# A transformer block kernel: the row buffers of its matmuls begin at other offsets from the weights, modulo 256 bytes

## The reference

```python
for l in range(DEPTH):                                   # DEPTH = 2
    need_ctx = l < DEPTH - 1                             # the context is carried on in layer 0 alone
    m  = silu(c) @ w_mod[l] + b_mod[l]                   # shifts, scales and gates
    o, oc = mix(modulate(x, g_mix[l]), modulate(xc, g_mix[l]), ...)
    x = x + gt1 * o
    x = x + gt2 * swiglu(modulate(x, g_ffn[l]), w_ffn_in[l], w_ffn_out[l])
    if need_ctx: ...                                     # the same for xc
return rmsnorm(x, g_final)

def mix(h, hc):                                          # four branches, gated and summed
    a_b, a_c, a_u, q, k, v, r_g, r_u, d_v, d_g, gl = split(h @ w_in)
    ys = (short_conv(a_b, a_c, a_u) @ w_a_out,  window_attention(q, k, v, kc, vc) @ w_b_out,
          (gelu(r_g) * rglru(conv(r_u))) @ w_c_out,  conformer_conv(d_v, d_g) @ w_d_out)
    return (sum_n sigmoid(gl_n) * ys_n) @ w_out
```

## Time and profile before

| | |
|---|---|
| median of three runs | 1960.27 us (1960.24 to 1960.73) |
| the profiled execution | 1960.5 us |
| its span, first instruction to last | 1958.7 us |
| granted TensorE clock, mean over the span | 0.997 |
| TensorE busy | 1930.0 us, 99% |
| VectorE, ScalarE, GpSimd busy | 72%, 46%, 41% |

### The profile page before, as it was taken

How to read it: one execution, slowest core, us unless ns; L and a number is a source line. 1 busy time by engine, 2 the same in 40 slices (tenths; PEclk the granted TensorE clock), 3 DMA queues, 4 the chain that set the end, 5 groups by cost and what they waited for, 6 DMA issues and landing times.

```text
span 1958.7 us, 29316 instructions
## 1 busy us (share of the span) xinstructions
PE 1930.0 (99%) x11006; PEld 1671.1 (85%) x11006; DVE 1416.5 (72%) x2475; ACT 908.0 (46%) x1439; POOL 812.0 (41%) x353
## 2 busy tenths in 40 slices
PE   7999999999999999999999999999999999999998
PEld 5778888888888888887888888878899999999998
DVE  5896666677789868798885544689788787645455
ACT  5787544232223343345222223599854435565443
POOL 1002322344444444344344444301647886454432
PEclk9999999999999999999999999999999999999999
DMA  8222211222232235534455442322334554544543
GB/s 344 86 86 81 92 65 65 85 88 107 86 105 88 100 138 216 192 129 170 174 219 192 190 175 83 140 78 106 130 108 151 180 186 174 193 172 172 194 174 127
DMA packets 38701, 276.25 MB, mean 141 GB/s; under 512 B 4416, under 2 KB 4416, under 8 KB 6336
## 3 DMA queue, kind: packets, MB, share of 16 engines
q1 hardware_dynamic: 38592, 274.77, 38.2%
HBM read 273.70 MB, written 1.05 MB: 140 GB/s over the span
## 4 chain that ended last, share of the span: by engine, by line
PE 81%; DVE 13%; ACT 3%; issue 2%; DMA 0%; POOL 0%; SPq 0%; DVEq 0%; ACTq 0%; POOLq 0%
PE PS L592 80%; DVE PS L1545 3%; DVE TMP L1542 1%; DVE TMP L1545 1%; ACT WH L1023 1%; DVE TMP L1548 1%; PE PS L905 1%; DVE S L1545 1%; ACT PS L1023 1%; DVE PS L1542 1%; DVE SM L1991 1%; DVE HL L1545 0%; DVE TMP L1864 0%; DVE ZL L1542 0%; DVE WL L1542 0%
## 5 line engine op out<-in xcount | busy, mean ns | idle before, releaser
L535 POOL TENSOR_TENSOR WL<-RAW,WH 128x1024 fp32r<-128x1024 f32 (+1 forms) x337 | 802.8, 2400 | 1122.9 <-ACT WH L1023 1122.9
L1023 ACT ACTIVATE WH<-RAW 128x1024 fp32r<-128x1024 f32 (+1 forms) x416 | 414.4, 1043 | 606.0 <-PE PS L592 571.4
L592 PE MATMUL PS<-HH,WH 128*128 128x512 f32 (+2 forms) x1968 | 680.7, 346 | 7.3 <-POOL WL L535 3.2
L592 PE MATMUL PS<-HH,WL 128*128 128x512 f32 (+2 forms) x1968 | 667.5, 339 | 0.0
L592 PE MATMUL PS<-HL,WH 128*128 128x512 f32 (+2 forms) x1968 | 666.9, 340 | 0.3 <-DVE HL L1545 0.3
L592 PE MATMUL PS<-ZH,WH 128*128 128x512 f32 (+1 forms) x1312 | 442.1, 337 | 3.7 <-DVE HL L1542 2.9
L592 PE MATMUL PS<-ZH,WL 128*128 128x512 f32 (+1 forms) x1312 | 441.0, 336 | 0.0
L592 PE MATMUL PS<-ZL,WH 128*128 128x512 f32 (+1 forms) x1312 | 439.3, 337 | 0.3 <-POOL ZL L559 0.3
L592 PEld LDWEIGHTS PS<-HH,WH 128*128 128x128 f32 x1968 | 373.0, 190 | 55.8 <-issue 8.2
L592 PEld LDWEIGHTS PS<-HL,WH 128*128 128x128 f32 x1968 | 372.6, 190 | 44.0 <-issue 3.8
L592 PEld LDWEIGHTS PS<-HH,WL 128*128 128x128 f32 x1968 | 373.0, 190 | 41.3
(11 more groups left out here) (210 smaller groups left out, 1740.3 us busy)
## 6 DMA issues: line engine op xcount, KB each, us to landing
RAW<-in_stream SPq DMA_DIRECT2D x200, 1024.0 KB, 4.8
CD<-in_modw SPq DMA_DIRECT2D x22, 1024.0 KB, 7.1
G<-in_modw SPq DMA_DIRECT2D x22, 1024.0 KB, 6.9
RAW<-in_stream SPq DMA_DIRECT2D x8, 768.0 KB, 4.2
CD<-in_lruw SPq DMA_DIRECT2D x2, 2048.0 KB, 11.7
X<-in_xT SPq DMA_DIRECT2D x2, 1024.0 KB, 7.1
S<-in_modw SPq DMA_DIRECT2D x2, 1024.0 KB, 12.9
RAW<-in_modw SPq DMA_DIRECT2D x1, 1024.0 KB, 19.8
```

What stands on the lines that cost most here:

```text
L535: nc.gpsimd.tensor_tensor(WL[:, a:b], RAW[:, a:b], WH[:, a:b].bitcast(F32), ALU.subtract)\
L592: return nc.tensor.matmul(out, lhs, rhs, start=start, stop=stop)
L1023: return nc.scalar.activation(out, in_, f, **kw)
```

## The change

The buffers are allocated in another order, and the second slot of `WH`, `WL` and `RAW` begins 8 words (32 bytes) later: `SLOT = SLAB + 8`, and `s * SLOT` wherever the code had `s * SLAB`. Small buffers (`PADA`, `BD2`, `AMP`, `EPST`) stand between the large ones. The offset of the rows from the weights thus becomes 64 bytes (`HH`, `HL`) or 224 bytes (`ZH`, `ZL`) where the slab is even, and 32 or 192 bytes where it is odd. No instruction is added, removed or moved on any of the five engines: apart from the shift of every line number by one, their programs read alike.

```diff
 SLAB = KC * 2 * P
+SLOT = SLAB + 8
 HALF = SLAB // 2
...
         MOD = sb("MOD", 2 * 48)
-        X = sb("X", KC * NT)
-        WH = sb("WH", 2 * SLAB, F32R)
-        WL = sb("WL", 2 * SLAB, F32R)
+        WH = sb("WH", SLOT + SLAB, F32R)
+        PADA, PADR = sb_and_rounded("PADA", 2 * GW)
+        WL = sb("WL", SLOT + SLAB, F32R)
+        BD2 = sb("BD2", KC)
+        HH = sb("HH", KC * UROW, F32R)
+        AMP = sb("AMP", 2 * 2 * KC)
+        HL = sb("HL", KC * UROW, F32R)
+        EPST = sb("EPST", 2)
         ZH = sb("ZH", KC * NT, F32R)
         ZL = sb("ZL", KC * NT, F32R)
-        HH = sb("HH", KC * UROW, F32R)
-        AMP = sb("AMP", 2 * 2 * KC)
-        SELB = sb("SELB", 32)
-        LC = sb("LC", 2 * 16)
-        HL = sb("HL", KC * UROW, F32R)
+        X = sb("X", KC * NT)
         S, SR = sb_and_rounded("S", KC * NT)
         CD = sb("CD", KC * NT)
-        RAW = sb("RAW", 2 * SLAB)
+        RAW = sb("RAW", SLOT + SLAB)
...
-                sp.dma_start(RAW[:, s * SLAB:s * SLAB + words], slab_of(stream, n)[:, 0:words]).then_inc(raw_loaded[s], 16)
+                sp.dma_start(RAW[:, s * SLOT:s * SLOT + words], slab_of(stream, n)[:, 0:words]).then_inc(raw_loaded[s], 16)
...
-                a = s * SLAB + k * 2 * P + t * P
+                a = s * SLOT + k * 2 * P + t * P
                 wh, wl = WH[:, a:a + P], WL[:, a:a + P]
```

More of the change, by code:

```diff
@@ L183, in build @@
         MOD = sb("MOD", 2 * 48)
-        X = sb("X", KC * NT)
-        WH = sb("WH", 2 * SLAB, F32R)
-        WL = sb("WL", 2 * SLAB, F32R)
+        WH = sb("WH", SLOT + SLAB, F32R)
[6 more added lines that the diff above has]
+        EPST = sb("EPST", 2)
         ZH = sb("ZH", KC * NT, F32R)
         ZL = sb("ZL", KC * NT, F32R)
-        HH = sb("HH", KC * UROW, F32R)
-        AMP = sb("AMP", 2 * 2 * KC)
-        SELB = sb("SELB", 32)
-        LC = sb("LC", 2 * 16)
-        HL = sb("HL", KC * UROW, F32R)
+        X = sb("X", KC * NT)
         S, SR = sb_and_rounded("S", KC * NT)
         CD = sb("CD", KC * NT)
-        RAW = sb("RAW", 2 * SLAB)
+        RAW = sb("RAW", SLOT + SLAB)
         TMP, TMPR = sb_and_rounded("TMP", 7 * NT)
         G = sb("G", KC * GW)
-        PADA, PADR = sb_and_rounded("PADA", 2 * GW)
         PRM = sb("PRM", DEPTH * NPRM)
@@ L204, in build @@
         SILC = sb("SILC", 32 * KC + 30)
+        SELB = sb("SELB", 32)
         SG = sb("SG", 2 * KC)
+        LC = sb("LC", 2 * 16)
         LT = sb("LT", 5 * 16)
-        EPST = sb("EPST", 2)
         WARM = sb("WARM", 1)
-        BD2 = sb("BD2", KC)
         SM = sb("SM", 3 * 14)
@@ L316, in build @@
         MOD_HOMES = [S[:, 0:SLAB], S[:, SLAB:2 * SLAB], CD[:, 0:SLAB], CD[:, SLAB:2 * SLAB],
-                     RAW[:, SLAB:2 * SLAB], TMP[:, 2 * NT:6 * NT], G[:, 0:SLAB], G[:, SLAB:2 * SLAB]]
+                     RAW[:, SLOT:SLOT + SLAB], TMP[:, 2 * NT:6 * NT], G[:, 0:SLAB], G[:, SLAB:2 * SLAB]]
         MOD_ORDER = [j + h * (MOD_FIRST // 2) for j in range(MOD_FIRST // 2) for h in range(2)]
@@ L533, in low @@
                 pool.wait_ge(hi_done[s], 2 * m + (h + 1))
-                a, b = s * SLAB + h * half, s * SLAB + (h + 1) * half
+                a, b = s * SLOT + h * half, s * SLOT + (h + 1) * half
                 nc.gpsimd.tensor_tensor(WL[:, a:b], RAW[:, a:b], WH[:, a:b].bitcast(F32), ALU.subtract)\
@@ L872, in _ @@
                     for k in range(KC):
-                        w0 = SLAB + k * 2 * P
+                        w0 = SLOT + k * 2 * P
                         h0 = k * NT + c * P
@@ L1028, in high @@
                 for h in halves:
-                    x = slice(s * SLAB + h * half, s * SLAB + (h + 1) * half)
+                    x = slice(s * SLOT + h * half, s * SLOT + (h + 1) * half)
                     fn(WH[:, x], RAW[:, x], ACT.Copy).then_inc(hi_done[s], 1)
@@ L1632, in low @@
                 dve.wait_ge(hi_done[s], 2 * m + 2)
-                x = slice(s * SLAB + half, s * SLAB + 2 * half)
+                x = slice(s * SLOT + half, s * SLOT + 2 * half)
                 tt(WL[:, x], RAW[:, x], WH[:, x].bitcast(F32), SUB).then_inc(lo_done[1][s], 1)
@@ L1810, in lows @@
                         dve.wait_ge(hi_done[s], 2 * m + (h + 1))
-                        x = slice(s * SLAB + h * HALF, s * SLAB + (h + 1) * HALF)
+                        x = slice(s * SLOT + h * HALF, s * SLOT + (h + 1) * HALF)
                         tt(WL[:, x], RAW[:, x], WH[:, x].bitcast(F32), SUB).then_inc(lo_done[h][s], 1)
```

## The result

| | before | with the change |
|---|---|---|
| median | 1960.31 us (1960.24 to 1960.73, 4 runs) | 1969.09 us (1968.54 to 1971.67, 4 runs) |
| ratio, 95% interval | | 1.0047 (1.0034 to 1.0061) |
| the profiled execution | 1960.5 us | 1971.67 us |
| its span | 1958.7 us | 1969.9 us |

What follows compares the result with a forecast made beforehand. TensorE bounds the kernel, busy for 1930.0 of 1958.7 us, through the distance between matmul starts. Terms of +15.3 and -4.9 us gave +10.4 us on 1960.5, so 1971 us; range 1922 to 1996 us, likeliest case 1965 to 1983.

Steps and rivals of the forecast that it cites:

- Only the distance can change; other engines cost 0.: All engines: the change moves only addresses, so only the distance between TensorE's matmul starts can change; other engines cost 0.
- 512 columns, +3.0 ns, +15.3 us.: 512-wide rows of H and Z by slab weights: 5088 matmuls, each 3.0 ns slower, +15.3 us; bounds -10.2 to +35.6 us.
- between offset 0 and 128 in proportion: 512-wide rows: loss scaled from 0 ns at offset 0 to +7 at 128; 32 bytes +1.75, 64 bytes +3.5.
- The witness at offset 128: Last `HH` by `WL` before the recurrence, with `CD` being loaded: 396 ns against 389, 7 ns more.
- the one at 160: Witness with `ZH` streamed and `CST` loaded: 391 ns, 2 ns more.
- 256 and 258 columns, -1.0 ns, -4.9 us.: Short rows: 4944 matmuls, each 1.0 ns faster, -4.9 us; bounds nothing and -15 us.
- The slab of 258 columns: Witness with offsets 0 to 120: distances of 120.0 ns where 120.8 was due, so short rows gain about 1 ns.
- The sum: Whole kernel: +15.3 - 4.9 = +10.4 us on the profiled execution's 1960.5 us, forecast as 1971 us.
- a steady distance with another value for one parity of slab: Sign of being wrong: a steady state appears at another value for one parity of slab and not the other.
- The rival of no change: Matmul distances: the loss could be a clash in time, not in addresses; 1960 us, chance 0.15.
- The rival of a gain: Matmul distances: at offset 0 both readers may meet most often; 1934, 1893 or 1827 us by share of loss removed; chance 0.39.
- The clearly slower rival: 512-wide rows: 64 and 192 bytes act like 128, +31 us, 1991 us; +70 us if short rows too; chance 0.13.

Runs made afterwards that it cites:

- the series: Kernels of their own, not the block: 96 matmuls per series, row offset from the weights varied, other engines idle; offset 0 settled at 226.7 ns for 512 columns in the first.
- the four programs of series: Separate kernels: 16 row buffers in 16-byte steps; two weight tensors; 64 offsets in 4-byte steps; four weight tensors. 4-byte steps gave nothing under 226.67 (512 columns) or 113.33 ns (256).
- The first series: Kernel of its own, weights at offset 0, 16 row buffers 0 to 240 bytes off, other engines idle; 228.9 to 236.7 ns at 512 columns apart from offset 0.

## Why the prediction came out right, and where its terms were off

- **Only the distance can change; other engines cost 0.** Right. The kernel with all other buffers moved took 1959.35 us, and the counts of instructions are those of before.
- **512 columns, +3.0 ns, +15.3 us.** Right in sign, too small: +4.9 ns in the mean, +25.0 us. The step that failed is "between offset 0 and 128 in proportion". 32 bytes have all of it, as much as 128 (233.3 in the series); 64 bytes are an exception with +2.2. The witness at offset 128 (7 ns) had the size right, 6.7 in the series; the one at 160 (2 ns) was too low by far, 7.7 in the series. A matmul beside a single float32 load says little of a settled series.
- **256 and 258 columns, -1.0 ns, -4.9 us.** Right in sign, mis-sized: -2.9 ns in the mean over the 4608 of the table, -13.4 us. The slab of 258 columns was a poor witness for the size: it kept 119.4 to 120.1 ns in the block's kernels before, after and with moved buffers alike. Its offset changes with each row, which may keep it from settling; no run tests that. (The prediction's 120.0 ns divides by 1167, one matmul taken off, where its 226.7 takes off two; by the start times it is 120.0 all the same.)
- **The sum.** +10.4 us forecast, +11.2 measured between the profiled executions, +8.8 by the medians. The two terms are off by 9.7 and 8.5 us in opposite directions. The closeness of the total is luck, and the changed forms show it: 394 to 396 ns where 392 was named, 279 where 282 was.
- **The chances and the signs.** The forecast had 0.33 and a gain 0.39, so the outcome was not the one held likeliest. One of the prediction's own signs of being wrong was met: a steady distance with another value for one parity of slab. 512-wide H rows are at 229.4 ns in even and 233.2 in odd slabs, 256-wide Z rows at 118.2 and 114.0. The prediction had the 512-wide rows 1.75 ns apart, with 64 bytes worse than 32; the runs show them 3.8 apart, with 64 the better.
- **The rival of no change** rested on a clash in time and not in addresses. It is refuted by the series: 226.7 to 240.0 and 113.3 to 126.7 ns with nothing changed but an address. The Trainium skill, "TensorE: Matmul & The Clock Gate", in what happens when a matmul is issued, has two independent read ports there; by that rule none of these runs would differ. They do, and the measurement decides. (The prediction's "every start here is a multiple of 32 bytes" leaves out the slab of 258 columns, whose rows begin every 2064 bytes.)
- **The rival of a gain** took offset 0 for the worst one. For 256 columns it nearly is, for 512 it is the best, and 51% of the matmuls are 512 wide. Its condition, a mean of the 512-wide distances under 227.7, was not met: by the table it is 232.0.
- **The clearly slower rival** had 64 and 192 act like 128. At 512 columns 192 does, and so do 32 and 224; 64 does not, and the short rows gave back 13.4 us and not 4.9.

What stays open: which mechanism makes the clash. The runs show its dependence on the offset and its steady states, not the cause. What decides between two steady states of one offset stays open too: the same pair changed with its place in the program, and the series just before it was not enough to tell. So does whether it is the rows' or the weights' start, 16 bytes off a multiple of 32, that gives a pair another distance.

## What to carry to other kernels

Where the matmuls follow one another with new weights each, measure the distance between starts against the offset of the streamed row from the weights, modulo 256 bytes, at the width that the kernel uses: two widths may want opposite offsets, and a change that suits one can cost the other more. Try the offset in the kernel itself, since an offset may have two steady states and the two starts count beside their difference: offset 112 won 16.6 us with the weights on multiples of 256 bytes and the rows moved, and 1.8 us with the weights moved to 144. A gain in TensorE's distance is paid out only as far as its inputs keep up.

## What the runs showed of the hardware

- At the full granted clock (0.997 to 1.000 over the four programs of series) the settled distances are whole multiples of 6.67 ns, 17 to 19 at 256 columns and 34 to 36 at 512, or means of patterns that lie between such multiples: 116.67 (17.5 times), 117.78 (17 and two thirds), 228.89 (34 and a third). 6.67 ns are 16 cycles of 2.4 GHz, and streaming alone at a column a cycle (106.7 and 213.3) would be 16 and 32 times. At offset 0 a matmul loses two such steps at either width; the best case at 256 columns loses one.
- The patterns repeat. The first series at offset 32 and 256 columns repeats 116, 117, 117 ns, the one at 128 bytes and 512 columns alternates between 229 and 238, and each repeat within the first series gave the same settled mean to 0.1 ns.
- One offset can hold two steady states (192 bytes, 256 columns: 113.33 and 117.78 ns), in the same buffers and within the same execution.
- With weights that begin 16 bytes off a multiple of 32 the distance is another at the same offset: 120.0 for 113.3 ns at 112 bytes and 256 columns, 230.0 or 233.3 for 226.7 at offset 0 and 512 columns, where the row begins 16 bytes off too.
